# A hybrid decoder layer: the index halves in another order, counts of the top-k search beside the projections on ScalarE (four tiles) and VectorE (two), and the last MLP blocks in pairs

## What is computed

```
proj = x @ w_in + b_in          # dq dk dv | iq ik iw | sq sk sv, rotary on q and k
# A: sparse attention, 8 query heads on one key/value head
rel   = relu(einsum('bthd,bsd->bths', iq, ik))
score = einsum('bths,bth->bts', rel, iw) * idx_scale      # causal
_, sel = top_k(score, 256)      # each query keeps 256 keys
o_dsa = softmax attention of dq on the kept keys
# B: window of 128, 8 query heads, 2 key heads, one learned sink per head
o_swa = banded softmax attention with sinks
h = LN1(alpha * x + [o_dsa, o_swa] @ w_o)
h = LN2(alpha * h + cross attention(h, mem: 256 tokens, 4 heads of 256))
h = LN3(alpha * h + square(relu(h @ w_up)) @ w_down)      # hidden 4096
```

## Time and profile before

| | us |
|---|---|
| median of 3 runs (lowest, highest) | 1660.16 (1659.97, 1660.46) |
| the profiled execution | 1660.99 |
| its span in the trace | 1659.2 |
| TensorE busy | 1530.4 (92%) |
| VectorE busy | 899.9 (54%) |
| ScalarE busy | 465.6 (28%) |
| GpSimd busy | 536.9 (32%) |

### The profile page before, as it was taken

How to read it: one execution, slowest core, us unless ns; L and a number is a source line. 1 busy time by engine, 2 the same in 40 slices (tenths; PEclk the granted TensorE clock), 3 DMA queues, 4 the chain that set the end, 5 groups by cost and what they waited for, 6 DMA issues and landing times.

```text
span 1659.2 us, 20746 instructions
## 1 busy us (share of the span) xinstructions
PE 1530.4 (92%) x7720; PEld 1301.2 (78%) x7720; DVE 899.9 (54%) x1827; ACT 465.6 (28%) x987; POOL 536.9 (32%) x540
## 2 busy tenths in 40 slices
PE   7999966988878999989999999999999999999993
PEld 6887756887768998778887788888888888888872
DVE  7568986779786433593427633333333333333348
ACT  3015436788664651121301211111111111110110
POOL 5242215666410003342233343333333333333100
PEclk9999987999876999999999999999999999999997
DMA  5564324555400004311110211111111111110002
GB/s 221 180 185 144 122 76 150 171 164 158 129 25 15 13 12 160 96 50 40 50 52 0 102 58 44 51 51 51 52 51 51 52 51 51 51 52 26 1 0 101
DMA packets 61331, 128.96 MB, mean 78 GB/s; under 512 B 6960, under 2 KB 34096, under 8 KB 53552
## 3 DMA queue, kind: packets, MB, share of 16 engines
q1 hardware_dynamic: 44208, 100.37, 18.3%
q10 hardware_dynamic: 17024, 27.27, 4.6%
HBM read 100.35 MB, written 27.26 MB: 77 GB/s over the span
## 4 chain that ended last, share of the span: by engine, by line
PE 76%; DVE 15%; issue 3%; ACT 3%; POOL 1%; DMA 1%; ACTq 0%; SPq 0%; DVEq 0%; POOLq 0%
PE banks L647 22%; PE banks L649 21%; PE banks L648 21%; PE banks L840 3%; PE banks L699 2%; PE banks L700 2%; DVE unread L1443 2%; PE banks L827 2%; ACT unread_wide L1017 2%; DVE h_buf L1752 1%; PE banks L849 1%; DVE bn L1738 1%; PE banks L796 1%; DVE trial L1420 1%; DVE h_buf L1761 1%
## 5 line engine op out<-in xcount | busy, mean ns | idle before, releaser
L633 POOL TENSOR_SCALAR w_hi<-raw 128x512 fp32r<-128x512 f32 x268 | 174.9, 680 | 1021.8 <-PE banks L649 688.4
L638 POOL TENSOR_TENSOR w_lo<-raw,w_hi 128x512 fp32r<-128x512 f32 x268 | 364.7, 1395 | 0.0
L1863 DVE TENSOR_TENSOR h_buf<-h_buf,banks 128x1024 f32<-128x1024 f32 x120 | 146.5, 1221 | 146.5 <-PE banks L649 146.5
L647 PE MATMUL banks<-w_hi,hid_hi 128*128 128x512 f32 x512 | 200.9, 392 | 7.9 <-DVE h_buf L1863 7.9
L647 PE MATMUL banks<-act_hi,w_hi 128*128 128x512 f32 x512 | 199.9, 390 | 1.7 <-DVE act_lo L1731 1.7
L648 PE MATMUL banks<-w_lo,hid_hi 128*128 128x512 f32 x512 | 200.4, 391 | 0.0
L649 PE MATMUL banks<-w_hi,hid_lo 128*128 128x512 f32 x512 | 200.2, 391 | 0.0
L649 PE MATMUL banks<-act_hi,w_lo 128*128 128x512 f32 x512 | 199.9, 390 | 0.0
L648 PE MATMUL banks<-act_lo,w_hi 128*128 128x512 f32 x512 | 199.8, 390 | 0.0
L1233 ACT ACTIVATE relu_buf<-banks 128x512 f32<-128x512 f32 x64 | 38.3, 599 | 549.6 <-PE banks L649 549.6
L1827 DVE TENSOR_TENSOR relu_buf<-relu_buf 128x512 f32<-128x512 f32 x64 | 45.0, 705 | 249.6 <-ACT relu_buf L1233 249.6
(11 more groups left out here) (178 smaller groups left out, 2805.5 us busy)
## 6 DMA issues: line engine op xcount, KB each, us to landing
raw<-w_up_dram SPq DMA_DIRECT2D x16, 1024.0 KB, 4.8
raw<-w_down_dram SPq DMA_DIRECT2D x16, 1024.0 KB, 4.8
q_tile<-qk_dram SPq DMA_DIRECT2D x176, 64.0 KB, 2.2
qk_dram<-q_hi ACTq DMA_DIRECT2D x28, 256.0 KB, 2.3
qk_dram<-roped ACTq DMA_DIRECT2D x28, 256.0 KB, 2.7
x_raw<-x_t_dram SPq DMA_DIRECT2D x8, 512.0 KB, 8.4
raw<-wk_mem_dram SPq DMA_DIRECT2D x4, 1024.0 KB, 5.9
raw<-wv_mem_dram SPq DMA_DIRECT2D x4, 1024.0 KB, 5.0
```

The lines of the kernel that those rows point to most:

```text
L633: pool.tensor_scalar(w_hi[s][:, col], raw[r % 2][:, col], 1.0, 1.0, ALU.mult, ALU.mult)\
L638: pool.tensor_tensor(w_lo[s][:, col], raw[r % 2][:, col], w_hi[s][:, col].bitcast(F32), ALU.subtract).then_inc(w_ready, 1)
L647: pe.matmul(dst, lh, rh, start=(first and n == 0), stop=False)
L1863: dve.tensor_tensor(h_buf[:, t, :], h_buf[:, t, :], ring_l[n % 2][:], ALU.add)\
```

## The change

- The iq units run as (m = 0, 1) for the first 512 tokens and then for the last ones. The index scores of tiles 2 and 3 run beside halves 10 and 11, those of tiles 7, 6, 5, 4 beside halves 14 to 17. The index key and the queries of tiles 2 and 3 are loaded as soon as four units are stored; the band keys follow; the sparse key is loaded after the last count.
- Four tiles (4 to 7) are counted by ScalarE and two by VectorE. One bit of each is counted beside every half from 18 to 27 and the rest in 21 of the band steps 0 to 30. Each wide tile has its own semaphore steps for count and bit. The first count and the turn of sign are made for one tile at a time behind its scores. The unread output of ScalarE's counts goes to SBUF throughout, where early ones went to PSUM.
- GpSimd subtracts (`split_roped`) for units 7 to 13. The rotation of the last half moves into band step 2.
- mem has a place of its own, is loaded behind the last index score and rounded before the last count beside the projections; memory products begin at step 2. Some buffers move.
- The hidden blocks 14 and 15 are ordered by token half, and their down products are made in pairs: 24 matmuls add up in PSUM before VectorE adds a tile once.

The core of the diff:

```diff
+UNITS = [(f, hf) for f in range(N_FF - 2) for hf in range(2)]
+N_SINGLE = len(UNITS)
+UNITS += [(f, hf) for hf in range(2) for f in (N_FF - 2, N_FF - 1)]
...
-    for chunk, what in ((C_IQ, "iq"), (C_SQ, "sq"), (C_DQ, "dq")):
+    units += [(C_IQ + m, ("iq", m), hf) for hf in range(2) for m in range(2)]
+    for chunk, what in ((C_SQ, "sq"), (C_DQ, "dq")):
...
-INDEX_HALF = 2 * N_ROPE_INDEX + 3
-BESIDE_HALF = INDEX_HALF + (NT - FIRST_TOPK_TILE)
-WIDE_HALF = BESIDE_HALF + 1
+INDEX_HALVES = {10: 2, 11: 3, 14: 7, 15: 6, 16: 5, 17: 4}
+INDEX_TILES = list(INDEX_HALVES.values())
+INDEX_START = {v: HEADS * j for j, v in enumerate(INDEX_HALVES)}
+N_INDEX_FIRST = 2
+BESIDE_HALF = max(INDEX_HALVES) + 1
+WIDE_HALF = BESIDE_HALF
+POOL_SPLIT = 7
...
-WIDE = N_SEL - 3
+WIDE = N_SEL - 4
+N_WIDE = N_SEL - WIDE
...
+COUNT_STEP = {WIDE_SPAN * j // WIDE_LEFT: TOP_BIT - N_EARLY - j for j in range(WIDE_LEFT)}
+LAST_COUNT_STEP = max(COUNT_STEP)
...
+NARROW_EARLY, BUDGET_BAND, BUDGET_DSA = 0.9, 1.8, 2.0
+WIDE_TILES = list(range(N_SEL - 1, WIDE - 1, -1))
+FIRST_PRODUCT = 2
...
-        band_prob = [place(f"band_prob{s}", [P, PAIR * BAND], F32, 183 + 2 * s) for s in range(4)]
-        kv_hi = [place(f"kv_hi{s}", [P, 2, MEM], F32R, 191 + 4 * s) for s in range(2)]
-        kv_lo = [place(f"kv_lo{s}", [P, 2, MEM], F32R, 193 + 4 * s) for s in range(2)]
+        band_prob = [place(f"band_prob{s}", [P, PAIR * BAND], F32, 64 + 4 * s) for s in range(4)]
+        mem_raw = place("mem_raw", [P, NK, MEM], F32, 120)
+        kv_hi = [place(f"kv_hi{s}", [P, 2, MEM], F32R, 120 + 4 * s) for s in range(2)]
+        kv_lo = [place(f"kv_lo{s}", [P, 2, MEM], F32R, 122 + 4 * s) for s in range(2)]
...
+                    load_key(1, index_keys_in)
+                    for j in range(N_INDEX_FIRST):
                         load_queries(j)
                 if c == C_DQ + 1:
-                    for j in range(3, NT - FIRST_TOPK_TILE):
+                    load_queries(N_INDEX_FIRST)
+                    for j in (2, 3):
+                        load_key(j, swa_keys_in)
...
+                    indexed(sp, i_full, len(IDX) - 1)
+                    sp.dma_start(mem_raw[:], a["mem_t"]).then_inc(mem_in, 16)
...
+                if C_MEM + 2 < c < C_MIX and not dsa_key_loaded \
+                        and (mem_unit(c - 3) > LAST_COUNT_STEP or c == C_MIX - 1):
+
+                    sp.wait_ge(wide_counted, (TOP_BIT + 1) * N_WIDE)
+                    load_key(0, dsa_keys_in)
+                    dsa_key_loaded = True
...
+            def split_roped(r):
+
+                for h in range(2):
+                    pool.wait_ge(q_rounded, 2 * r + h + 1)
+                    pool.tensor_tensor(roped[r % 2][h][:].bitcast(F32R), roped[r % 2][h][:],
+                                       q_hi[h][:].bitcast(F32), ALU.subtract).then_inc(q_split_late, 1)
+
+            split_before = {C_DQ: (7,), C_DQ + 1: (8, 9), C_MEM: (10, 11), C_MEM + 1: (12,), C_MEM + 2: (13,)}
             for c in range(1, N_CHUNKS):
                 s, n = slot_of(c), columns_of(c)
-
-                r = raw_of(c)
-                landed = r // 2 + 1 - (r > C_MEM and r % 2 == C_MEM % 2)
-                pool.wait_ge(raw_in[r % 2], 16 * landed)
+                for r in split_before.get(c, ()):
+                    split_roped(r)
...
+                    pe.wait_ge(swa_keys_in, 16 * 16)
+                    for n in range(len(IDX) - 3, len(IDX)):
+                        indexed(pe, i_free, n)
+                if t == NT and h == 0:
+                    pe.wait_ge(dsa_keys_in, 16 * 8)
...
+            def down_pair(u):
+
+                parts = []
+                for v in (u, u + 1):
+                    c = C_MLP + 2 * UNITS[v][0] + 1
+                    parts.append((hid_hi[v % 2], hid_lo[v % 2]) + tuple(parts_of(c, 2)))
+                    pe.wait_ge(w_ready, PIECES * c)
+                pe.wait_ge(hid_ready, 2 * u + 2)
+                for tt in range(4):
+                    n = L_DOWN + 4 * N_SINGLE + 4 * ((u - N_SINGLE) // 2) + tt
+                    freed(pe, l_free, n)
+                    tok = slice(tt * P, (tt + 1) * P)
+                    for half in range(2):
+                        col = slice(half * HALF, (half + 1) * HALF)
+                        for v, (hh, hl, wh, wl) in enumerate(parts):
+                            if tt == 0 and half == 0 and v == 1:
+                                pe.wait_ge(hid_ready, 2 * u + 4)
+                            mm = exact(ring_l[n % 2][:, col],
+                                       [(hh[:, j, tok], hl[:, j, tok], wh[:, j, col], wl[:, j, col])
+                                        for j in range(2)], first=(v == 0), final=(v == 1))
...
+                up(u + 1)
                 down(u)
+            for u in (N_SINGLE, N_SINGLE + 2):
+                up(u + 1)
+                if u == N_SINGLE:
+                    up(u + 2)
+                down_pair(u)
...
+            def count_wide(k):
+
+                for m, c in enumerate(WIDE_TILES):
                     i = FIRST_TOPK_TILE + c
-                    act.activation(unread[c - WIDE][:, 0:(i + 1) * P], score[i][:], ACT.Sign,
+
+                    act.wait_ge(trial_ready, (TOP_BIT - k) * N_WIDE + m + 1)
+                    if k < TOP_BIT:
+
+                        act.wait_ge(wide_counted, (TOP_BIT - k - 1) * N_WIDE + m + 1)
+                    act.activation(unread_wide[m][:, 0:(i + 1) * P], score[i][:], ACT.Sign,
                                    bias=trial[:, c:c + 1].bitcast(F32), accum_out=count[:, c:c + 1])\
                         .then_inc(wide_counted, 1)
...
+            for r in range(len(ROPE)):
+                for v in (2 * r, 2 * r + 1):
+                    if v == N_HALVES - 1:
+                        round_mem()
+                    if wide_bit_beside_rope(v) is not None:
+                        count_wide(wide_bit_beside_rope(v))
+                    for n in index_own(v):
+                        rectify_scores(n)
+                    if v % 2 == 0 and r > POOL_SPLIT:
+                        store_low(r - 1)
+                if r < len(ROPE) - 1:
+                    move_roped(r)
...
+            def prepare(c):
+
+                i, col = FIRST_TOPK_TILE + c, slice(c, c + 1)
+                width = (i + 1) * P
+                tally(c, ALU.is_ge, 0.0, None)
+                dve.wait_ge(dve_step, written[-1])
+                chain(dve.tensor_scalar(negative[:, col], count[:, col], float(TOPK), None, ALU.is_lt))
+                signed = then(dve.tensor_scalar(sign[:, col], negative[:, col], -2.0, 1.0, ALU.mult, ALU.add))
+                ranked = then(dve.tensor_scalar(minus_rank[:, col], negative[:, col],
+                                                float(2 * TOPK - 1 - width), -float(TOPK), ALU.mult, ALU.add))
+                dve.wait_ge(dve_step, signed)
+                flipped = then(dve.tensor_scalar(score[i][:], score[i][:], sign[:, col], None, ALU.mult))
+                dve.wait_ge(dve_step, ranked)
+                if c < WIDE:
+                    then(dve.memset(trial[:, col], 1 << TOP_BIT))
+                    dve.wait_ge(dve_step, steps[0])
+                    set_at[c] = steps[0]
...
+                def find(m, c):
+                    dve.wait_ge(wide_counted, (TOP_BIT - k) * N_WIDE + m + 1)
+                    found_at[c] = then(find_refused(c, k, offset[:, c:c + 1]))
+
+                def apply(m, c):
+                    dve.wait_ge(dve_step, found_at[c])
+                    set_next(c, k).then_inc(trial_ready, 1)
+                    if k == 0 and m == N_WIDE - 1:
                         wide_set[0] = True
...
+            for v in range(last_half):
+                if v - 1 in INDEX_HALVES:
+                    prepare(INDEX_HALVES[v - 1] - FIRST_TOPK_TILE)
+                if v >= BESIDE_HALF:
+
+                    pending.extend(set_wide(wide_bit_beside_rope(v)))
+                    if v % 2:
+                        flush(2)
+                        select_for(NARROW_EARLY)
+                        flush()
+                    else:
+                        select_for(NARROW_EARLY)
+                        flush(2)
+                rotate_and_split(v)
+                flush()
+            split_mem()
+            pending.extend(set_wide(wide_bit_beside_rope(last_half)))
+
             for n in range(NS + ND + 4):
+                if n == 2:
+                    rotate_and_split(last_half)
+                    move_place()
...
+                if n >= 2:
+                    select_for(BUDGET_BAND if n < NS else BUDGET_DSA)
+                    flush()
```

380 lines of the change are left out of this document (175 added, 205 removed).

## The result

The changed kernel takes 1648.76 us (median of 4 runs, 1647.16 to 1651.08) against 1660.07 for the kernel before, measured beside it: ratio 0.9933, 95% interval 0.9916 to 0.9950. Its profiled span is 1647.4, 11.8 us less than the 1659.2 of before. The forecast was 36.5 us less. The direction was right, the size was not, and the time lies above the range of 8 in 10.

What follows compares the result with a forecast made beforehand. The front's loss was placed between 120 and 540 us, the end in VectorE's LayerNorm chain. Sparse attention's 20 us and the tail's 16.5 off the 1659.2 span gave 1622.7, plus 1.0: 1623.7 us; 8-in-10 range 1597 to 1645.

Steps and rivals of the forecast that it cites:

- What bounds the kernel: Whole kernel: the front's whole loss lies between 120 and 540 us; TensorE at full clock from 620 to 1600.
- Tail: Last two hidden blocks multiplied together: the end is TensorE's end plus the last tile's chain, 16.5 us less (13 to 19).
- Projections 10 to 17: Index scores start five halves earlier, VectorE's preparation spread between them: half 17 rotated at 172 us (170 to 176).
- I take 0 to 2 us: Projections 10 to 17: allowance for queries coming late after being split, stored and loaded again.
- Projections 18 to 27: A count of four tiles beside each half: 14.8 us per pair of halves (13 to 16), half 25 at 232.
- The first band steps: Up to band step 3: the wait for mem changes its name rather than going; step 3 at 263.5 against 265.19.
- Steps 3 to 31: Band steps: ScalarE becomes the busiest engine at 5.16 us a step; 5.55 a step, 155.4 us, step 31 at 419.
- over 90%: Sign for the band steps: ScalarE this busy from step 3 to 420 us, TensorE waiting for its copies and exponentials.
- From step 31 to the sparse attention: Nine steps after the counts end: 39 us against 49.2, first sparse step at 458, 1 us less.
- Sparse attention: First 24 sparse steps 58 us, last 24 72; last step at 588 to 590 against 609.75, 20 us less.
- (c): Rival: front stays as it was, ScalarE taking all that VectorE gives; 1638 to 1644 us, chance 0.15.
- (b): Rival, slower: bit round trips between ScalarE and VectorE in steps 0 to 31 starve TensorE to 1.2 GHz; chance 0.05.

Runs made afterwards that it cites:

- index_later: The changed kernel with the four wide index score tiles beside halves 15 to 18 instead of 14 to 17; 0.9940 of the kernel before.
- prepare_late: The changed kernel with the first count and turn of sign of the four wide tiles in one row behind half 17; 0.9942 of the kernel before.
- no_narrow: The changed kernel with index scores beside halves 15 to 20, the sparse key loaded early and no narrow-tile counts beside the projections; 0.9880 of the kernel before.
- count_less: The changed kernel with ScalarE counting only 128 of 640 columns of the fourth wide tile in the band steps; 0.9902 of the kernel before.
- key_early: The changed kernel with the sparse key loaded ahead of the band steps' counts, which write elsewhere; 0.9889 of the kernel before.

## Why the prediction was wrong, point by point

**What bounds the kernel.** Right. The loss of the front lay between 120 and 540 us and now begins with the index scores at 92, and everything from 620 on stayed as it was but for the tail.

**Tail.** Right: 16.5 forecast (13 to 19), 17.8 by the two profiles, 14.4 to 17.8 by four. The last add stands 12.8 us ahead of the end (forecast 12.7), the adds are 5.86, 6.23 and 5.85 apart, the wait for the hidden half is 1.44.

**Projections 10 to 17.** This is the first step that failed: 172 was forecast for half 17, 176 at most, and it was 188.6. From half 9 on it is 98.4 us where 80 were planned, 18.4 more, since half 9 came 1.9 us ahead of the plan. TensorE's time accounts for all of it: it was busy 82.9 us where the plan had 75, and idle 15.5 where it had 5.

The idle time first. 4.4 us of it are waits for queries, 1.06 for those of tile 2 and 3.38 for those of tile 7. "I take 0 to 2 us" was the mis-sized term: the way from the split through ScalarE's store to DRAM and SP's load back stood in the prediction as "split, stored and loaded again" without a duration. By the trace VectorE's last subtraction ends at 120.0, SP issues from 122.11 and the first product starts at 127.45. With the slow clock behind the wait this came to 6.3 us in the half where it fell (index_later). 9.7 us are waits for VectorE's sums. The preparation was put "between score sums, where three score slots let TensorE run ahead about 4 us"; TensorE waited 4 times, 8.9 us, for the first sum of a tile, and prepare_late shows that 7.4 us of halves 14 to 17 go when the preparation is moved out of them, only to come back behind them. The last 1.4 us are a wait for the rotation of half 12.

Then the busy time. The same stages have some 78.2 us of TensorE where each ran at a clock of 1.00 (29.0 for halves 9 to 13 here, 15.3 for tile 7 in index_later, 12.0, 11.1 and 10.7 for the others in prepare_late). So about 3 of the 8 us more are work that the sum had too small, and about 5 are the granted clock, 0.84 in the half of tile 7 and 0.94 in the two last ones.

Contention with GpSimd has a share in the waits for VectorE that no run isolates. VectorE's additions and subtractions on two SBUF operands took up to 1.77 us each in that stretch: the two subtractions that the queries of tile 7 had to wait for took 3.48 us together beside a weight split of GpSimd, and one addition is slow just where GpSimd begins the split that the change gave it. VectorE's timeline after at half 15, and GpSimd's:

```profile
160.38 0.69 DVE L1456 TENSOR_TENSOR roped<-roped,rot_part 128x512 f32<-128x512 f32 x1
...
161.89 1.73 DVE L1462 TENSOR_TENSOR roped<-roped,rot_part 128x512 f32<-128x512 f32 x1
```

```profile
161.81 1.26 POOL L664 TENSOR_TENSOR roped<-roped,q_hi 128x512 fp32r<-128x512 f32 x1 [42.35 <-ACT q_hi L1072]
```

The prediction had 1.10 us for this and left it out of its sum. The Trainium skill, SBUF — State Buffer, Who interferes with whom, says that VectorE and GpSimd lock each other out of one shared pair of ports; the trace agrees with it, and 1.73 against 0.69 us for the same kind of instruction is more than the earlier trace rows showed. The splits themselves take GpSimd 1.26 to 1.30 us (forecast 1.5) and GpSimd has the time for them, as forecast: it had waited 42 us before this one. But they are not free. In every pair of halves from 15 to 25 one addition of VectorE is slow in this way (1.73 to 1.77 us, six times), so of the two subtractions of 0.68 us that a pair took off VectorE about 1.05 us come back.

**Projections 18 to 27.** Right to 0.1 us, in part by luck: 14.8 forecast for a pair, 14.86, 14.84 and 14.85 measured (halves 19 to 25). The chain through three engines is the one that was forecast, and the two counts of 3.9 us are in it. But two terms were off and cancel, and the stated terms add up to 15.0, not 14.8. From the rotation to the first count 4.0 was forecast and it is 5.2 (203.40 to 208.57), since the slow addition beside GpSimd is there too (1.76 us at 205.69). The low stores, about 1 us in the sum, cost nothing: ScalarE's queue issues them while the count runs.

```profile
208.57 1.15 ACT L1098 ACTIVATE unread_wide<-score,trial 128x1024 bf16<-128x1024 f32 x1 [0.46 <-ACT q_hi L1072]
208.96 0.88 ACTq L1087 DMA_DIRECT2D qk_dram<-roped  x2
```

That VectorE's narrow counts are a part of the chain is borne out by no_narrow (13.6).

**The first band steps.** Right: 31.5 forecast from half 25 to step 3, 32.0 measured.

**Steps 3 to 31.** Right in length: 155.4 forecast, 154.6 measured. That ScalarE sets the pace is supported by count_less and not proven. The prediction's ScalarE work was 144.4 with 11 us of issuing; the trace has 131.3 busy, 85% and not the "over 90%" of the signs. The mean of 5.52 us a step is 0.36 above the 5.16 of that sum, where 0.4 was added; a spread of 6 us between two traces of the same band work makes a hit to 0.8 us partly luck.

**From step 31 to the sparse attention.** The second step that failed: 39 forecast, 51.1 measured. "A load of 8 parts, about 4 us once" was right for the issue (3.6 us), and 39 was what the work takes; what was left out is how late the load starts. TensorE is done with what it can do without this key at 435.76. ScalarE's last count ends at 437.7, 3.2 us behind the start of step 31, SP issues from there to 441.3, and TensorE goes on at 444.44. In the 5 us that follow the granted clock is 0.53 while the memory product runs, and in the 5 us behind those it is 1.00. key_early removes 11.7 us with that one dependence. The prediction's own sentence on this wait named SP's queue behind it and never the consumer of the key.

**Sparse attention.** Right: 58 + 72 forecast, 58.3 + 71.9 measured, though its parts (41 at full clock, 8.6 for VectorE, 8 for the clock) weren't measured one by one. It only started 27.6 us later than planned: 16 of the first failed step, 12 of the second.

**Sum.** 16.6 + 12.1 = 28.7 too late; 2.7 won back in the other stages leave the 48th sparse step 26.0 late; the tail's 1.3 more makes 24.7, which is 36.5 - 11.8.

**Rivals and signs.** (c), the front stays as it was, had the time next to the measured one (1638 to 1644 for 0.15) but not the mechanism: the pairs and the band steps took what the forecast had, not what (c) gave them. (b) was about band steps falling to 1.2 GHz; 0.89 was the mean clock there. The rival that was missing is "the index scores start before their queries are back, the preparation has no cover and the key load is late"; the range, 1597 to 1645, ended 3.8 us short. "Wrong would be the forecast if step 31 came before 400 or after 435" didn't catch it: step 31 came at 434.5, already 15.5 us late, and the second failed step lies behind it.

## What to carry to other kernels

Give each transfer between a write and its reader its own line in the sum, with the time from the last producer's instruction to the first consumer's instruction, both ways through the queue; a trip out to DRAM and back that is forecast at nothing needs the name of the work that hides it. A load that is held behind the last of something is late by the length of its own issue plus its landing whenever its reader stands next in line. When work is moved to an earlier place, ask what waits for it there: here the early index scores bought three bits of counting, which the band steps took back at 2.5 to 8.4 us, and moving the scores back brought step 3 some 8 us forward.
